# Two panels at a time behind five norms, with fillers in the gaps, a third panel buffer and an earlier table load

## What is computed

```python
xn = rms_norm(x, g_norm1[l]) * (1 + scale1) + shift1
p = xn @ w_in[l]
...
u = rms_norm_2(h, pre_norm[layer])
q, k, v, g_ret, cb, cc, cx, g_conv = split_cols(u @ w_in, EVEN_SPLITS)
...
h = h + rms_norm_2(y, post_norm[layer])
```

## Time and profile before

| | |
|---|---|
| median of 3 runs | 2334.73 us (2334.53 to 2340.07) |
| the profiled execution | 2335.68 us, span 2333.6 us |
| TensorE busy | 2191.2 us, 94% of the span |
| VectorE / ScalarE / GpSimd busy | 1211.2 / 725.2 / 652.0 us |
| mean granted TensorE clock | 0.976 of full speed |
| HBM traffic | 91 GB/s over the span |

### The profile page before, as it was taken

How to read it: one execution, slowest core, us unless ns; L and a number is a source line. 1 busy time by engine, 2 the same in 40 slices (tenths; PEclk the granted TensorE clock), 3 DMA queues, 4 the chain that set the end, 5 groups by cost and what they waited for, 6 DMA issues and landing times.

```text
span 2333.6 us, 26283 instructions
## 1 busy us (share of the span) xinstructions
PE 2191.2 (94%) x10898; PEld 1764.2 (76%) x10898; DVE 1211.2 (52%) x1548; ACT 725.2 (31%) x1073; POOL 652.0 (28%) x283
## 2 busy tenths in 40 slices
PE   5898897999999999799989999998999999899997
PEld 5785576888888888685568888876778888778655
DVE  5996577566555665587454302346332344432265
ACT  2323433222112221424542212223253222234542
POOL 2100002223332233200044434433224444423302
PEclk9999998999999999899999999999999999989998
DMA  7312132334333333121023323322223333212301
GB/s 262 122 46 90 37 136 64 108 127 137 111 105 125 122 129 113 59 73 73 1 86 100 111 79 93 113 83 82 81 64 89 92 100 100 90 46 58 101 1 54
DMA packets 60165, 213.57 MB, mean 92 GB/s; under 512 B 6672, under 2 KB 10384, under 8 KB 59792
## 3 DMA queue, kind: packets, MB, share of 16 engines
q1 hardware_dynamic: 57888, 206.92, 27.6%
q10 hardware_dynamic: 2160, 4.98, 0.6%
HBM read 209.77 MB, written 2.10 MB: 91 GB/s over the span
## 4 chain that ended last, share of the span: by engine, by line
PE 85%; DVE 8%; ACT 3%; issue 2%; DMA 1%; POOL 1%; SPq 0%; ACTq 0%; DVEq 0%
PE prod L544 73%; PE misc L582 2%; PE prod L719 1%; PE prod L687 1%; DMA ring<-in_wmod 1%; PE prod L595 1%; PE prod L774 1%; ACT operand_hi L1034 1%; PE misc L903 1%; PE misc L647 1%; PE misc L798 1%; PE prod L624 1%; DVE work L1435 1%; PE misc L786 1%; DVE operand_lo L1407 1%
## 5 line engine op out<-in xcount | busy, mean ns | idle before, releaser
L523 POOL TENSOR_TENSOR wlo<-ring,whi 128x1024 fp32r<-128x1024 f32 (+3 forms) x256 | 610.4, 2385 | 1591.5 <-ACT whi L981 1591.5
L544 PE MATMUL prod<-operand_hi,whi 128*128 128x512 f32 (+1 forms) x2208 | 735.4, 373 | 36.2 <-DVE operand_lo L1423 14.1
L544 PE MATMUL prod<-operand_hi,wlo 128*128 128x512 f32 (+1 forms) x2208 | 725.1, 368 | 0.0
L544 PE MATMUL prod<-operand_lo,whi 128*128 128x512 f32 (+1 forms) x2208 | 721.3, 367 | 0.0
L981 ACT ACTIVATE whi<-ring 128x1024 fp32r<-128x1024 f32 (+3 forms) x284 | 293.5, 1034 | 736.5 <-PE prod L544 736.5
L544 PEld LDWEIGHTS prod<-operand_hi,whi 128*128 128x128 f32 x2208 | 381.8, 190 | 127.9 <-issue 28.2
L544 PEld LDWEIGHTS prod<-operand_hi,wlo 128*128 128x128 f32 x2208 | 380.6, 190 | 68.7
L544 PEld LDWEIGHTS prod<-operand_lo,whi 128*128 128x128 f32 x2208 | 379.4, 190 | 69.4 <-issue 2.4
L1473 DVE CUSTOM_DVE_ANT_0 mod_junk<-modw,silu_c,par 128x1024 bf16<-128x1024 f32 x68 | 123.7, 1820 | 79.2 <-DMA modw<-in_wmod 78.6
L544 PE MATMUL prod<-hidden_hi,whi 128*128 128x512 f32 (+1 forms) x528 | 160.6, 358 | 0.0
L544 PE MATMUL prod<-hidden_lo,whi 128*128 128x512 f32 (+1 forms) x528 | 160.4, 358 | 0.0
(11 more groups left out here) (244 smaller groups left out, 2173.8 us busy)
## 6 DMA issues: line engine op xcount, KB each, us to landing
ring<-in_w SPq DMA_DIRECT2D x224, 512.0 KB, 3.6
modw<-in_wmod SPq DMA_DIRECT2D x68, 512.0 KB, 3.7
ring<-in_w SPq DMA_DIRECT2D x32, 704.0 KB, 4.9
ring<-in_wmod SPq DMA_DIRECT2D x28, 512.0 KB, 4.7
dft<-in_dftx SPq DMA_DIRECT2D x8, 512.0 KB, 5.2
resid<-in_xt SPq DMA_DIRECT2D x1, 3072.0 KB, 13.7
ring<-in_w SPq DMA_DIRECT2D x12, 192.0 KB, 2.3
ret_r<-in_decay ACTq DMA_DIRECT2D x8, 256.0 KB, 2.9
```

What stands on the lines that cost most here:

```text
L523: nc.gpsimd.tensor_tensor(wlo[j % 2][:, 0:w], ring[PLACE["panel", j] % RING][:, 0:w], whi[j % 2][:, 0:w].bitcast(F32), ALU.subtract).then_ ...
L544: mm = pe.matmul(G[b][:, t0:t0 + tn], w[v][:, k * P:(k + 1) * P], a[:, t0:t0 + tn], start=(i == 0 and q == 0), stop=(i == g.kc - 1 and q = ...
```

## The change

Five parts. (1) In the five stages of `TWO_FIRST` panels 0 and 1 are issued together, panel 1 one chunk behind panel 0; the third panel has high and low buffers of its own, so that it needn't wait for panel 0's. (2) ScalarE's copies of panel 1 and, ahead of its place, panel 2 stand behind the root (at oin's pair of norms one behind each root). (3) `root(load=True)` puts a one-element Sqrt into a scrap buffer ahead of the waits of the root, and with it the table load. (4) `rms` issues filler matmuls (`keep_busy`: 256 columns of a constant times ones, into the PSUM bank M1, read by nobody): 4 ahead of the sums, 3 behind them, 8 (at 512 tokens 5) behind the transposes; not at the first norm, and no leading 4 at the residual norm ahead of oin. (5) VectorE's `panel_low` also waits for the panel before to have its low part.

```diff
+TWO_FIRST = ("fin00", "win1", "fin10", "eqk", "oin")
+THIRD = {GEMM[name].j0 + 2: name for name in TWO_FIRST}
...
+        third = {}
+        for name, hi_at, lo_at in (("fin00", 9 * NT, 14 * NT), ("win1", NT, 3 * NT), ("eqk", 16 * NX, 18 * NX), ("oin", 0, 13 * NX)):
+            third[name] = [at(f"{which}_{name}", DC * P, F32R, region + 4 * o) for which, o in (("whi", hi_at), ("wlo", lo_at))]
+        third["fin10"] = third["fin00"]
+
+        def whi_of(j):
+            return third[THIRD[j]][0] if j in THIRD else whi[j % 2]
...
-                for p in range(begin, g.n if panels is None else panels):
+                two = name in TWO_FIRST
+                for i in range(g.kc + 1 if two else 0):
+
+                    for p in range(2):
+                        if 0 <= i - p < g.kc:
+                            panel(name, p, high, low, width(p) if callable(width) else width, i - p, i - p + 1, ready=first_ready)
+                for p in range(2 if two and after is not None else 0):
+                    after(p)
+                for p in range(2 if two else begin, g.n if panels is None else panels):
...
+            def keep_busy(count):
+
+                for _ in range(count):
+                    pe.matmul(M1[:, 0:256], ones, con[:, 0:256], start=True, stop=True)
...
             def rms(nchunks, width, sq_tiles, by_head=False, free=None, total=None):
+
+                first = n["rope"] == 0
+                wait(pe, rope_done, n["rope"])
+                wait(pe, ret_copied, 8 if n["rope"] > 8 else 0)
+                keep_busy(4 if total is not None and not first else 0)
                 sum_squares(nchunks, width, sq_tiles, by_head, total)
+                keep_busy(0 if first else 3)
                 spread_roots(width, sq_tiles, free)
+                keep_busy(0 if first else 5 if width == NX else 8)
...
                     if norm_follows and p == g.n - 1:
                         after(p)
-                        high(j + 2)
                     else:
-                        high(j + 2)
+                        if j + 2 not in THIRD:
+                            high(j + 2)
...
+                if load:
+
+                    nc.scalar.activation(scrap[:, 0:1], eps, ACT.Sqrt)
                 act.wait_ge(sq_used, n["sq"])
...
-                root(width, 1024)
+                root(width, 1024, load=True)
                 if l == 0 and which == 0:
                     high(0)
                     high(1)
+                else:
+                    for p in (1, 2):
+                        high(GEMM[("win", "fin")[which] + str(l) + "0" * which].j0 + p)
...
-            root(NX, 1024)
+            root(NX, 1024, load=True)
+            high(GEMM["eqk"].j0 + 1)
+            high(GEMM["eqk"].j0 + 2)
...
+                dve.wait_ge(lo_ready, j)
                 dve.wait_ge(hi_ready, j + 1)
```

More of the change, by code:

```diff
@@ L268, in build_program @@
         rootT = sb("rootT", 24)
+        scrap = sb("scrap", 1)
         region = top[0]
@@ L365, in build_program, with wlo_of @@
         assert max(endA, endB) <= SBUF_END - 10 * DC * P and endD <= SBUF_END - 8 * DC * P
+        third = {}
[4 more added lines that the diff above has]
+            return third[THIRD[j]][0] if j in THIRD else whi[j % 2]
+        def wlo_of(j):
+            return third[THIRD[j]][1] if j in THIRD else wlo[j % 2]
         def ps(name, width):
@@ L522, in _ @@
                     pool.wait_ge(hi_ready, j + 1)
-                    nc.gpsimd.tensor_tensor(wlo[j % 2][:, 0:w], ring[PLACE["panel", j] % RING][:, 0:w],
-                                            whi[j % 2][:, 0:w].bitcast(F32), ALU.subtract).then_inc(lo_ready, 1)
+                    nc.gpsimd.tensor_tensor(wlo_of(j)[:, 0:w], ring[PLACE["panel", j] % RING][:, 0:w],
+                                            whi_of(j)[:, 0:w].bitcast(F32), ALU.subtract).then_inc(lo_ready, 1)
         @block.tensor
@@ L533, in panel @@
                 j = g.j0 + p
-                b, v = BANK[j], j % 2
+                b = BANK[j]
                 if first == 0:
@@ L541, in panel @@
                         ready(k)
-                    for q, (w, a) in enumerate(((whi, high(k)), (whi, low(k)), (wlo, high(k)))):
+                    for q, (w, a) in enumerate(((whi_of(j), high(k)), (whi_of(j), low(k)), (wlo_of(j), high(k)))):
                         for t0, tn in [s for s in SEGS if s[0] < width]:
-                            mm = pe.matmul(G[b][:, t0:t0 + tn], w[v][:, k * P:(k + 1) * P], a[:, t0:t0 + tn],
+                            mm = pe.matmul(G[b][:, t0:t0 + tn], w[:, k * P:(k + 1) * P], a[:, t0:t0 + tn],
                                            start=(i == 0 and q == 0), stop=(i == g.kc - 1 and q == 2))
@@ L980, in high @@
                     landed(act, ("panel", j))
-                    nc.scalar.activation(whi[j % 2][:, 0:w], ring[PLACE["panel", j] % RING][:, 0:w], ACT.Copy).then_inc(hi_ready, 1)
+                    nc.scalar.activation(whi_of(j)[:, 0:w], ring[PLACE["panel", j] % RING][:, 0:w], ACT.Copy).then_inc(hi_ready, 1)
             def stage(name, evac=None, after=None, norm_follows=False, panels=None):
@@ L1011, in square, with root @@
                 n["sq"] += c == DC - 1
-            def root(width, dim, heads=1, source=None):
+            def root(width, dim, heads=1, source=None, load=False):
                 source = MM if source is None else source
+                if load:
+                    nc.scalar.activation(scrap[:, 0:1], eps, ACT.Sqrt)
                 act.wait_ge(sq_used, n["sq"])
@@ L1320, in _ @@
             stage("eout1", None, lambda p: square(p, Y[:, p, :], NX, W[0], W[1], lambda c: freed(act, GEMM["eout1"].j0 + c)), True)
-            root(NX, 1024)
+            root(NX, 1024, load=True)
+            high(GEMM["oin"].j0 + 1)
             rms([X[:, c, 0:NX] for c in range(DC)], NX, W, lambda c: act.wait_ge(resid_ready, c + 1))
             root(NX, 1024)
+            high(GEMM["oin"].j0 + 2)
             normed_high(XH, DC, W)
@@ L1395, in panel_low @@
                 w = KC_OF[j] * P
+                dve.wait_ge(lo_ready, j)
                 dve.wait_ge(hi_ready, j + 1)
-                nc.vector.tensor_tensor(wlo[j % 2][:, 0:w], ring[PLACE["panel", j] % RING][:, 0:w], whi[j % 2][:, 0:w].bitcast(F32),
+                nc.vector.tensor_tensor(wlo_of(j)[:, 0:w], ring[PLACE["panel", j] % RING][:, 0:w], whi_of(j)[:, 0:w].bitcast(F32),
                                         ALU.subtract).then_inc(lo_ready, 1)
```

## The result

The median of the runs fell from 2334.64 us to 2306.24 us (four of each); the ratio is 0.9864, 95% interval 0.9836 to 0.9892, which is 25 to 38 us. The four executions of the changed kernel lie at 2298.33, 2303.66, 2308.83 and 2309.78 us. The profiled one is the fastest: a span of 2296.5 us, 37.1 less than in the profile before.

The account below looks back on a forecast made before the run. TensorE was taken as the bound, 85% of the chain, idle at the norms. Gains of 5.5 + 5.7 + 3.8 + 2.4 + 4.4 + 0.5 = 22.3 us, less 1.0, gave 2334.73 - 21.3 = 2313.4 us, range 2306 to 2322.

Parts of the forecast that it names:

- fin00: Norm at fin00: gain of 5.5 us taken, between 6.9 with the clock held and 3.4 if it falls.
- win1: Norm at win1: both panels done at 984.8 instead of 990.5, a gain of 5.7 us.
- eqk: Norm at eqk: gain of 2.4 us taken, GpSimd's subtractions for panels 1 and 2 now running one behind the other.
- oin: Norms ahead of oin: net 0.3 us ahead of the interleaving, then panels done at 2070.4 against 2074.9; gain 4.4 us.
- what had been taken off for friction: Whole sum: 1.0 us off for satisfied waits in interleaved panels, the added wait ahead of panel_low and the scrap activation.
- fin10: Norm at fin10: shift of 1.1 us, panels ending at 1218.0 instead of 1222.0; gain 3.8 us.
- the other bound (3.4): fin00's norm if the clock falls all the same: chunk 1 at 397.2, end at 413.2, gain 3.4 us.
- the shift of 1.5 us with every dummy hidden: At win1: 0.65 + 0.83 us earlier, from the copy moved behind root and transposes at full clock.
- the price that I had named for a fallen clock: The 3 dummies behind the sums at half clock: 2.6 us against 1.37 us of cover at fin00.
- the signs of being wrong: New profile: dummies at half clock, TensorE waiting for panel 2's wlo, or panel 2 for panel 0's bank over 0.5 us.
- the two orders that I had worked out: At eqk: low(0) slips between GpSimd's two subtractions, gain 2.6 us, or waits for both, gain 1.6.
- The rival of the dummies at half clock: At all norms, dummies at 1.2 GHz delay the panels in TensorE's in-order queue: 2337 us in all; chance 0.05.

Follow-up runs that it names:

- The second profile: Profile from running the changed kernel once more, unaltered; that run's median was 2300.0 us, ratio 0.9847.
- the one with the shifted operand: Changed kernel with operand_hi and operand_lo moved by 64 bytes to an odd multiple of 64; median 2332.78 us, ratio 0.9992.
- placement alone: Kernel before with only the unused scrap column added, moving the buffers behind it by 64 bytes; median 2332.52 us, ratio 0.9986.
- the run with one break: Changed kernel with 7 and 5 dummies ahead of the sums and a 1-column matmul at the start of fin00's panel 3; ratio 0.9881.
- placement and two breaks: Kernel before with scrap's 64 bytes and 1-column matmuls at the start of fin00's panels 3 and 4; median 2328.46 us, ratio 0.997.

## Why the prediction was right and wrong

**The norms were right in sum, in part by luck.** 21.3 us were forecast and 21.3 found, but the terms missed by +1.3 (fin00), -2.1 (win1), +0.5 (eqk) and -0.7 (oin), and the 1.0 that came short is what had been taken off for friction, which nothing showed. The second profile gives 20.3 for the five norms where the first gives 20.8. fin10 gave 3.85 against 3.8, and within 0.1 of that in every kernel with interleaving and dummies but the one with the shifted operand (3.57). fin00 gave 6.75 against 5.5, because the clock held there. Other profiles show what I had as the other bound (3.4): with one short fall of the clock the norm took 30.7 to 31.4 us, with two 33.0 (the run without the early load), which is 3.9 of gain.

**win1 gave 3.56 against 5.7.** The step that failed is the shift of 1.5 us with every dummy hidden: chunk 0 came 12.40 us behind the last panel matmul, 0.47 later than before. The interleaving behind it gave 4.0 of the 4.2 that were put, and the four afac operations took 0.52 us where 2.56 stood. The dummies ahead of the sums ended 1.52 us before them, the clock was at 0.50 at 948, and the 3 dummies behind the sums took 2.91 us. VectorE's copy ended at 949.16, the transposes began at 950.54. This is the price that I had named for a fallen clock, but not charged here; dummies at half clock were also one of the signs of being wrong. It is not there in every execution: the six profiles with 4 dummies ahead and no breaks have 27.82, 26.83, 27.28, 26.18, 26.30 and 26.22 us, the three with 7 dummies 26.17, 26.16 and 26.16. Where the low stretch fell later, under running panels, or not at all, the norm gave 5.1 to 5.2, close to the forecast.

**eqk** gave 2.94 against 2.4, by the first of the two orders that I had worked out: low(0) slipped in ahead of GpSimd's second subtraction (0.91 us), low(1) lay beside it for 2.07 us. The Trainium skill ("SBUF — State Buffer", SBUF: two separate sides) has the later of two such operations wait for the whole of the first; the row of 2.07 agrees, as low(1) ended 0.54 us behind GpSimd's. In five profiles, in which the clock fell 10.7 to 12.2 us behind the norm's start, the norm took 23.2 to 23.3 us, a gain of 1.5.

**oin** gave 3.74 against 4.4: the clock fell in the sums and the 3 dummies behind them took 2.91 us, both as forecast in kind, and the transposes then took 1.06. Chunk 0 came 0.05 us later than before where 0.3 earlier was put, and the interleaving gave 3.8 of 4.1.

**The rival of the dummies at half clock** came true in parts, at win1 and oin, 1 to 1.5 us each, and never near its sum.

**What was wrong is what I left out.** This is the step that failed in the forecast of the whole. The sum took every stage between the norms at its time before, and priced scrap as one small activation among the 1.0 us of friction. scrap's column moves the region by 64 bytes. That gave 6.1 us by itself in the hidden and mix stages (placement alone: 226.7 ns; the change without the shift: 233.3), and it took away what had held fout00 and all behind it at 176.7 ns, so that up to 10.6 us more can come, by chance, in each execution. 21.3 + 6.1 = 27.4 us off 2334.6 is 2307.2; with the fast pace throughout, 2296.6. The profiled execution of the run with one break, at 176.7 ns throughout, took 2306.71; those of the changed kernel, at 173.3, took 2298.33 and 2300.48. The 2.2 us between these two lie in the attention between win1's norm and fin10's. The windows of it, the second profile's, then the first's:

```profile
969.60:1179.20 209.60, 198.77 (x1046) 144.89 (x1045) 138.21 (x203) 79.98 (x126) 21.50 (x9) 0.98 0.19 59
```

```profile
970.60:1177.80 207.20, 196.13 (x1046) 142.63 (x1045) 138.26 (x203) 79.95 (x126) 21.49 (x9) 1.00 0.19 59
```

The kernel is the same, yet this stretch took 2.3 us more (209.65 against 207.32), with two short falls of the clock in it; the norms took 0.5 more in sum, and the part ahead of them 0.8 less.

**What stays open** is what draws the pace at 768 tokens. Shown: the two paces, each kept through more than 530 us; that a 1-column matmul can change it. In both profiles that were fast in fin00 with an unaligned hidden_hi, fout00 and all behind it were slow; no aligned profile changed its pace without a break. By their times, 16 of 29 executions with interleaving and placement are fast, 2 of 23 with placement alone or with dummies, 6 of 12 with placement and two breaks, none of the 76 of the kernel before (none is below 2330). Only one execution of each run has a profile, so the rest is inferred from groups of times, and these are not crisp: 2306.71 us had 176.7 ns throughout, so the executions at 2303 to 2305 that are counted at the shorter pace are the least certain. By these counts interleaving raises the odds; I could not show by what, nor set the pace on purpose.

**A better version.** With 7 and 5 dummies ahead of the sums three executions of five lie at 2297.1 to 2298.3, level with the best of the changed kernel or 1 us below it, and win1's norm stayed at its best in all three profiles with 7. In the median it can't be told from the changed kernel: the pace's draw moves single executions by 11 us.

## What to carry to other kernels

Before a change is priced stage by stage, look at what it does to the addresses of buffers behind a new one: the base of a matmul's operands at a multiple of 128 bytes was worth as much here as the largest term of the reasoned change. If executions of one kernel fall into groups, compare the pitch of the matmuls in the same dense stage before explaining the difference by what was edited. A dummy behind a small operation is priced at the low clock too, since one short fall of the clock, which comes at other places in other executions, makes it run past its cover: here 1.3 us at win1 and 1.5 at oin.

## What the hardware showed unexpectedly

- A stream of 512-column matmuls with fresh weights each runs at 226.7 ns, and at 233.3 when the moving operand stands at an odd multiple of 64 bytes: 6.7 ns each. Where only the weights stood so (third panels of win1, fin10 and oin in the kernel without the shift) it was 228.9 ns. Both at an odd multiple was not run. The Trainium skill ("SBUF — State Buffer", Operand start alignment) asks only for a multiple of the element's size and says that its runs timed nothing; every address here obeys that, and the time still differs.
- The Trainium skill ("TensorE: Matmul & The Clock Gate", Wait — 56ns, not 53.3ns?) gives 215.7 ns start to start for 512 columns at the full clock. No stream of 512-column matmuls with fresh weights each came below 226.7 here, and for this case the measured figure holds.
- 512 and 256 columns in turn have two stable paces, 1040 and 1060 ns for six matmuls, with everything aligned and the clock at 1.00.
